# Input projections of a two-block transformer kernel: from single fp32 products to three fp32r products of split operands

## The reference

```python
c_act = jax.nn.silu(c)
mod = c_act @ w_ada[l] + b_ada[l]                 # 6 x 1024 numbers
shift1, scale1, gate1, shift2, scale2, gate2 = jnp.split(mod, 6, axis=-1)
h = modulate(x, norm1_g[l], shift1, scale1)       # rms_norm(x) * (1 + scale1) + shift1
proj = h @ w_in[l]                                # (256 x 1024) @ (1024 x 2320)
q_g, k_g, v_g, a_lr, r_g, q_s, k_s, v_s = jnp.split(proj, split_at, axis=-1)
log_a = log_sigmoid(a_lr @ w_gla_alpha[l] + b_gla_alpha[l]) / GLA_GATE_TEMP
o_gla = gla_mixer(q_g, k_g, v_g, log_a)           # gated linear attention, 4 heads
o_swa = swa_mixer(q_s, k_s, v_s, swa_sinks[l])    # sliding window attention, 8 heads
```

## Time and profile before

| | us |
|---|---|
| three runs | 1850.57, 1854.89, 1855.41 |
| median | 1854.89 |
| profiled execution, its own time | 1855.27 |
| its span | 1853.7 |
| share of TensorE matmul / VectorE / ScalarE / GpSimd busy | 91% / 58% / 45% / 24% |
| the stretch of the input projections, slot 0 to slot 17 | 42.2 to 111.0 |

### The profile page before, as it was taken

The page is one execution under the profiler, slowest core; times in us unless marked ns, Lnnn a source line. Parts: engine busy times, 40 slices in busy tenths (PEclk is TensorE's granted clock), DMA queues, the critical chain, the costliest instruction groups (busy, mean ns, idle before and its releaser), DMA issues.

```text
span 1853.7 us, 34170 instructions
## 1 busy us (share of the span) xinstructions
PE 1682.4 (91%) x11384; PEld 1517.6 (82%) x11384; DVE 1069.6 (58%) x2448; ACT 835.0 (45%) x1767; POOL 448.0 (24%) x399
## 2 busy tenths in 40 slices
PE   5975889999999999999999977589999988899996
PEld 3872789998999999778887755479999848699996
DVE  5537569916777732555555542666555624765554
ACT  3214445565444445555555531355555403555553
POOL 4102367886666677000000010000000000010000
PEclk8975899999999999999999987699999987999999
DMA  8851234553444445555555531125555462045552
GB/s 312 326 187 46 78 128 149 178 177 127 141 136 138 145 159 181 192 190 190 190 191 191 191 128 46 45 81 170 182 182 182 145 216 91 1 154 183 184 182 91
DMA packets 80752, 287.63 MB, mean 155 GB/s; under 512 B 10080, under 2 KB 11408, under 8 KB 80432
## 3 DMA queue, kind: packets, MB, share of 16 engines
q1 hardware_dynamic: 72016, 257.30, 42.0%
q0 software_dynamic: 7344, 26.35, 3.8%
q10 hardware_dynamic: 1328, 3.15, 0.5%
HBM read 284.14 MB, written 2.62 MB: 155 GB/s over the span
## 4 chain that ended last, share of the span: by engine, by line
PE 83%; DVE 9%; ACT 3%; issue 2%; DMA 2%; POOL 1%; SPq 0%; DVEq 0%; ACTq 0%; POOLq 0%
PE pu L527 12%; PE pu L528 12%; PE pu L529 12%; PE pacc L586 6%; PE pacc L584 6%; PE pacc L585 6%; PE pacc L527 3%; PE pacc L528 3%; PE pacc L529 3%; PE pu L499 3%; PE pu L509 2%; PE pacc L631 2%; PE pm L800 2%; PE pn L800 2%; PE pn L517 1%
## 5 line engine op out<-in xcount | busy, mean ns | idle before, releaser
L343 ACT ACTIVATE ring_hi<-ring 128x512 fp32r<-128x512 f32 x880 | 505.6, 622 | 524.6 <-PE pu L529 288.1
L350 DVE TENSOR_TENSOR ring_lo<-ring,ring_hi 128x512 fp32r<-128x512 f32 x592 | 386.0, 694 | 336.4 <-ACT ring_hi L343 336.2
L527 PE MATMUL pu<-Xh,ring_hi 128*128 128x256 f32 x1472 | 431.0, 293 | 23.7 <-DVE Xl L1382 5.3
L528 PE MATMUL pu<-Xl,ring_hi 128*128 128x256 f32 x1472 | 419.6, 285 | 0.0
L529 PE MATMUL pu<-Xh,ring_lo 128*128 128x256 f32 x1472 | 419.3, 285 | 0.0
L350 POOL TENSOR_TENSOR ring_lo<-ring,ring_hi 128x512 fp32r<-128x512 f32 x288 | 370.2, 1307 | 130.8 <-ACT ring_hi L343 130.1
L527 PEld LDWEIGHTS pu<-Xh,ring_hi 128*128 128x128 f32 x1472 | 285.1, 194 | 30.2 <-issue 18.1
L528 PEld LDWEIGHTS pu<-Xl,ring_hi 128*128 128x128 f32 x1472 | 285.8, 194 | 0.2
L529 PEld LDWEIGHTS pu<-Xh,ring_lo 128*128 128x128 f32 x1472 | 285.2, 194 | 0.0
L584 PE MATMUL pacc<-ring_hi,vh 128*128 128x512 f32 x512 | 200.5, 392 | 0.0
L586 PE MATMUL pacc<-ring_lo,vh 128*128 128x512 f32 x512 | 200.5, 392 | 0.0
(11 more groups left out here) (328 smaller groups left out, 2619.0 us busy)
## 6 DMA issues: line engine op xcount, KB each, us to landing
ring<-in_weights SPq DMA_DIRECT2D x488, 512.0 KB, 3.3
big<-in_ada POOLq DMA_DIRECT2D x40, 512.0 KB, 6.2
bias_row<-big ACTq DMA_DIRECT2D x1, 1536.0 KB, 6.8
XT<-in_xT ACTq DMA_DIRECT2D x1, 1024.0 KB, 8.4
scr<-in_ada POOLq DMA_DIRECT2D x2, 512.0 KB, 12.4
tk<-in_ada POOLq DMA_DIRECT2D x2, 512.0 KB, 14.1
early_h<-in_ada POOLq DMA_DIRECT2D x2, 512.0 KB, 16.2
early_l<-in_ada POOLq DMA_DIRECT2D x2, 512.0 KB, 17.7
```

The source lines that it names most:

```text
L343: nc.scalar.activation(ring_hi[:, n % 2, half], ring[:, n % RING, half], ACT.Copy).then_inc(s["split_hi"], 1)
L350: api.tensor_tensor(ring_lo[:, n % RING, half], ring[:, n % RING, half], ring_hi[:, n % 2, half], ALU.subtract).then_inc(s[LOW[name][0]], 1)
L527: mm(out, ring_hi[:, n % 2, w], xh, start=start, stop=False, skip_group_check=True)
L528: mm(out, ring_hi[:, n % 2, w], xl, start=False, stop=False, skip_group_check=True)
```

## The change

`w_in` joins the split matrices. `project` and `project_tokens` give way to `split_project` and `split_tokens` for these 18 slots; `HTf` is split chunk by chunk into `Xh` (ScalarE) and `Xl` (VectorE); ScalarE makes the high parts of each slot just ahead of an `evac`, and VectorE the low parts. The modulation rows that VectorE summed in one call of 18 are now summed one by one behind a `split_low`, 13 in the loop of slots 5 to 17, 6 after `gla_ops`, then 2 and 3 in two later places. `early_h` moves into `ring_hi` and `early_l` into memory that the decays use later. `split_high` waits for no used slot when n is 0 or 1.

```diff
-        early_h = sb("early_h", [P, 2 * D], F32, where["Xh"])[:, :]
-        early_l = sb("early_l", [P, 2 * D], F32, where["Xl"])[:, :]
+        early_h = sb("early_h", [P, 2 * D], F32, where["ring_hi"])[:, :]
+        early_l = bigf[:, early_at:early_at + 2 * D]
...
-            act.wait_ge(s["slots_used"], tick(g, BODY, n - 1))
+            if n > 1:
+                act.wait_ge(s["slots_used"], tick(g, BODY, n - 1))
...
+            def split_tokens(name, k, e):
+                n = SLOT[name] + k
+                pe.wait_ge(s["evacs"], e - 1)
+                for tt in range(TT):
+                    rows = slice(tt * P, (tt + 1) * P)
+                    out = entry(e)[:, rows]
+                    for c in range(C):
+                        if tt == 0 and c % 4 == 0:
+                            split_ready(name, k, c // 4, None)
+                        w = slice(c * P, (c + 1) * P)
+                        mm(out, Xh[:, c, rows], ring_hi[:, n % 2, w], start=(c == 0), stop=False, skip_group_check=True)
+                        mm(out, Xl[:, c, rows], ring_hi[:, n % 2, w], start=False, stop=False, skip_group_check=True)
+                        last = mm(out, Xh[:, c, rows], ring_lo[:, n % RING, w], start=False, stop=(c == C - 1),
+                                  skip_group_check=True)
+                last.then_inc(s["slots_used"], 1)
+
+            def split_project(name, k, e):
+                n = SLOT[name] + k
+                if e >= 2:
+                    pe.wait_ge(s["evacs"], e - 1)
+                for c in range(C):
+                    if c % 4 == 0:
+                        split_ready(name, k, c // 4, None)
+                    if k == 0:
+                        pe.wait_ge(s["hx_lo"], c + 1)
+                    last = three(entry(e), n, slice(c * P, (c + 1) * P), Xh[:, c, :], Xl[:, c, :], c == 0, c == C - 1)
+                last.then_inc(s["slots_used"], 1)
...
-                project(SLOT["w_in"] + i, USE["w_in"] + i, HTf)
+                split_project("w_in", i, USE["w_in"] + i)
...
-                project_tokens(SLOT["w_in"] + i, USE["w_in"] + i, HTf)
+                split_tokens("w_in", i, USE["w_in"] + i)
...
+                act.wait_ge(s["h_chunks"], c + 1)
+                f(Xh[:, c, :], HTf[:, c, :], ACT.Copy).then_inc(s["hx_hi"], 1)
+            split_high(act, "w_in", 0)
+            split_high(act, "w_in", 1)
...
+                if i + 2 < 18:
+                    split_high(act, "w_in", i + 2)
                 if i < 2:
                     evac(n_slot, qg[:, i, :], src, scale=float(GK) ** -0.5)
...
+            for c in range(C):
+                dve.wait_ge(s["hx_hi"], c + 1)
+                v.tensor_tensor(Xl[:, c, :], HTf[:, c, :], Xh[:, c, :], ALU.subtract).then_inc(s["hx_lo"], 1)
+            split_low(dve, v, "w_in", 0)
+            split_low(dve, v, "w_in", 1)
             dve.wait_ge(s["h_chunks"], C)
             v.memset(stats[:, 0:1], 0.0).then_inc(s["normed"], 1)
+            split_low(dve, v, "w_in", 2)
+            split_low(dve, v, "w_in", 3)
             dve.wait_ge(s["la_parts"], 1)
             step(v.scalar_tensor_tensor(la, zb, 0.0, zln, ALU.min, ALU.subtract))
             for hp in range(HP):
                 last = v.tensor_tensor_scan(B[:, hp, :], scanmask, la[:, hp, :], 0.0, ALU.mult, ALU.add)
             step(last)
+            split_low(dve, v, "w_in", 4)
...
-            modulation(2 * C, 18)
+            for i in range(5, 18):
+                split_low(dve, v, "w_in", i)
+                modulation(2 * C + i - 5, 1)
...
-            modulation(2 * C + 18, 6)
+            modulation(2 * C + 13, 6)
...
             last.then_inc(s["states_ready"], 1)
+            modulation(2 * C + 19, 2)
...
             last.then_inc(s["gla_o_ready"], 1)
+            modulation(2 * C + 21, 3)
```

More of the change, by code:

```diff
@@ L62 @@
 for _name, _k in _COUNTS:
-    if _name in ("w_out", "peer_q", "peer_u", "peer_v", "a_o", "mlp0", "kv", "b_in", "b_o", "mlp1"):
+    if _name in ("w_in", "w_out", "peer_q", "peer_u", "peer_v", "a_o", "mlp0", "kv", "b_in", "b_o", "mlp1"):
         SPLIT[_name] = _n
@@ L107 @@
     OUTNO.append((OUTNO[-1] if OUTNO else -1) + (1 if _u[4] else 0))
-SEMS = """c_loaded x_loaded cols_loaded small_loaded xn_ready h_scaled h_chunks h2_sq h2_sum h2_scaled h2_hi h2_lo consts_made casts_made c_silu ada_used chain_dve chain_act chain_pool slots_used evacs alr_psum
+SEMS = """c_loaded x_loaded cols_loaded small_loaded xn_ready h_scaled hx_hi hx_lo h_chunks h2_sq h2_sum h2_scaled h2_hi h2_lo consts_made casts_made c_silu ada_used chain_dve chain_act chain_pool slots_used evacs alr_psum
 alr_copied z_psum squares sums roots normed la_parts ex_ready ex_done gla_ops kl_psum kl_copied gla_scores
@@ L216, in build @@
         mid_lo = -(-at["front"] // T)
+        early_at = at["front"]
         zb, zab, zln, la = (area("front", HP, T) for _ in range(4))
```

## The result

The changed kernel takes 1863.05 us, median of 8 runs (1861.52 to 1868.85), against 1852.63 us for the kernel before (8 runs, 1850.57 to 1859.34). The ratio is 1.0057 with a 95% interval of 1.0040 to 1.0074: 10.4 us slower, by medians, where the forecast was 8.2 more and 1863.1 in all. The profiled execution of the changed kernel took 1862.77 us with a span of 1861.1.

A forecast was written before the change was run, and what follows sets the result against it. TensorE, 91% busy, was taken as the bound, mostly `w_in` matmuls from 42.3 to 111 us. Slot 17 ending at 119.2 against 111.0 gave +8.2 on 1855.3, 1863.5, less 0.4 to the median: 1863.1 us, range 1855 to 1873.

The forecast's parts named there:

- Token slots: Slots 13 to 17: 48 products at 112 ns each, set by weight loads, 5.38 us a slot, 9.0 us more for five.
- Rival A: Slots 13 to 17: products cost as float32, 223 ns, 10.7 us a slot, 1890 us in all; chance 0.12.
- rival B: Slots 13 to 17: products cost what their columns do, 60 to 80 ns, 1851 to 1855 us in all; chance 0.07.
- Wide slots: Slots 0 to 12: 2.88 us each against 3.454, 7.5 us less over 13 if TensorE never waits.
- Start of slot 0: First `w_in` slot: starts at 44.9, 2.6 us later than before, behind ScalarE's and VectorE's splitting of the activations.
- half clock: Slots 0 and 2, after TensorE's gaps: low clock for 15 products in 3.2 us, so 4.3 us a slot instead of 2.88.
- Slots 2 and 5: Slot 2 starts at 57.9 (before 53.37), waiting for ScalarE's `evac` 0; slot 5 at 69.7 (before 65.5), behind VectorE's decays.
- Transfers and moved rows: Slot loop at 364 GB/s, 89% of the most, without stall; modulation rows moved into VectorE's waiting time; both taken as nothing.
- Rival C: Start costs less: full clock in slots 0 and 2, loads of 107 ns; up to 4 us less, 1859; chance 0.17.
- the case of a slot 0 at full clock: End of slot 17: 118.2 if slot 0 runs at full clock, else 119.6; 119.2 was taken.

The follow-up runs named there:

- wide slots alone: The changed kernel with slots 13 to 17 multiplied as float32 again and not split, slots 0 to 12 as changed; 1855.63 us, ratio 1.0008.
- half columns: The changed kernel with each product of slots 13 to 17 streaming 64 columns instead of 128, weight loads unchanged; 1887.72 us in one run.
- wide values: The changed kernel with the four value slots laid out so each loaded activation piece meets 512 columns, 12 products a slot instead of 48; 1853.72 us, ratio 0.9998.
- early-emptying run: The changed kernel with ScalarE making slot 2's high part and emptying slot 0 before the gate; 1861.84 us, ratio 1.0034.

## Why the prediction was right

**Token slots, the largest term: right.** (The forecast's "16 records become 48 products" is a slip: it is 16 products of two records, 32 in all.) 5.38 us a slot forecast, 5.36 measured; 26.9 us for five, 26.8 measured; 8.9 us of loss. The mechanism, a load of about 112 ns that hides the columns, was tested from both sides: half the columns change nothing at full clock (112 ns), a quarter of the loads halves the time of a slot. Rival A (223 ns) and rival B (60 to 80 ns) are excluded by the same rows. The fp32r loads are recorded at 192 ns and cost 112, like float32 ones.

The Trainium skill's figure for a load, columns / 1.2 ns (TensorE: Matmul & The Clock Gate, section LDWEIGHTS), agrees to 5 ns at full clock. At granted clock 0.50 it does not: 213 ns against 106.7. There the measurement decides. The Trainium skill, TensorE: Matmul & The Clock Gate, section Weight-path perf modes, gives the fast path to loads of 128 columns that are not FP32. By the 112 ns fp32r stands on FP32's side there.

**Wide slots: right.** 2.88 us each, as in `w_out`.

**Start of slot 0: right in place, with a term too small.** 44.9 forecast, 44.26 measured. The half clock lasted through the whole slot, 24 x 0.213 = 5.1 us, and not the 4.3 taken from the stretch ahead of `w_out`. The same held for slot 2. The length of the slow stretch had been priced by one example. What hid this is that ScalarE needed 0.94 us for each pair of HTf and Xh, not 1.05, so that slot 0 started 0.6 us sooner than forecast. How long the slow stretch lasts is a matter of the execution too: in the kernels with the wide slots alone, half columns and wide values, whose start is the same, slot 2 began at 57.1 to 57.3 and slot 5 at 69.5 to 69.7, where the forecast had 57.9 and 69.7.

**Slots 2 and 5: right in mechanism.** Slot 2 waited for ScalarE's emptying of slot 0 (57.9 forecast, 58.47 measured), slot 5 for VectorE's low part behind the decays (69.7 forecast, 71.67 measured). So slot 5 started 6.2 us later than in the kernel before instead of 4.2. Of the 2.0 too few, 0.6 had built up by slot 2. Another 0.9 is slot 2 itself (5.25 us instead of 4.3), which the high and low parts of slot 4, and so the decays, waited for in turn. The last 0.5 lies in the hand-overs: 1.0 us instead of 0.65 from the end of slot 2 to VectorE's low part of slot 4, and 0.1 more ahead of slot 5. VectorE's decays took what was forecast (4.87 us).

**Transfers and moved rows: right, nothing.** Landing took 3.4/4.8/6.5 us, under the 7.3 that the forecast allowed. The three waits of ScalarE were hidden. The rows moved into the attention lay in waiting time: the 2 from 144.59 to 147, ahead of a 2.64 us wait, and the 3 from 150.54 to 154, ahead of a 2.83 us wait.

**Rival C**, a shorter start, was not the case in the profiled execution, but the early-emptying run shows that slot 0 can run at 1.00 behind the same wait. It is a matter of the single execution, which the forecast had said no row could tell.

The sum: 10.7 = 6.2 (slot 5's start) - 4.6 (eight shorter slots) + 8.9 (tokens) + 0.2 (the rest). The forecast's 8.2 lacked the 2.0 at slot 5 and the 0.4 taken off for the case of a slot 0 at full clock. That the total of 1863.1 was nevertheless met within 0.1 us is luck: it started from 1854.9, the median of 3 runs, and over 8 runs the kernel before has 1852.63, 2.3 less, about as much as the slowdown was too small.

## What to carry to other kernels

Before a matmul is cut into more passes of a cheaper type, count its weight loads. Three fp32r products beat one float32 product where the moving side is wide enough to cover the load: at 256 columns 24 x 120 ns against 16 records x 216 ns (two records for each float32 product). At 128 columns they lose, 48 x 112 against 32 x 112, half as many again at the same price. Widths between these were not measured. Where the columns are the weights, lay them out so that one load meets 512 of them.

When work is inserted ahead of an `evac` or behind a serial chain, look at the first few slots. There is no slack in them yet, and a few us of waiting can cost half clock on top (slots 0 and 2 here, but not slot 5). Here the start ate all that 13 faster slots had gained.

## What the runs showed of the hardware that was not expected

- Products of 64 columns, issued without any idle time, did not hold the clock: the granted clock was 0.50 from 95.6 us to the end of the token slots, so that the kernel with less work took 1887.72 us. The same happens at the 24 column products of the second block in all twelve traces, the kernel before's among them. With 128 columns the clock stayed at 1.00 for 27 us.
- A load of 128 columns of 4-byte weights costs 112 ns at clock 1.00 and 213 ns at 0.50, 1.9 times as much. Loads of 64 x 64 let products start 63 ns apart at 0.50.
- The same wait ahead of the same slot (1.95 and 1.96 us, slot 0) was followed by clock 0.50 in one execution and 1.00 in another.
